# Waits of GpSimd on quarters of a weight buffer in a three-layer transformer kernel

## The reference

```python
for l in range(DEPTH):                    # first_block, DEPTH = 2
    h = rmsnorm(x, norm_w[l])
    proj = jnp.einsum("bsd,de->bse", h, w_in[l])       # 2048 -> 6160
    ...                                    # ssd, conformer, differential attention
    y = jnp.concatenate([y_ssd, y_cfm, y_att], axis=-1)
    x = x + jnp.einsum("bse,ed->bsd", y, w_out[l])
...
u = rmsnorm_2(h, g_pre)                   # hybrid_layer
z = u @ w_in                              # 2048 -> 9216
...                                       # banded attention, recurrence
y = jnp.concatenate([y_att, y_hg], axis=-1).astype(h.dtype) @ w_out
h = h + rmsnorm_2(y, g_post)
gate = jax.nn.sigmoid((h @ w_pg).astype(f32))
e = (p_l @ w_pp).astype(f32)
h = h + rmsnorm_2((gate * e).astype(h.dtype), g_ple)
```

## Time and profile before

| what | value |
| --- | --- |
| median of 3 runs | 3264.14 us (3263.51 to 3265.61) |
| span of the profiled execution, first to last instruction | 3255.8 us |
| the profiled execution's own time | not given beside its span |
| TensorE busy | 3045.4 us |
| GpSimd busy | 1950.9 us |
| VectorE busy | 1788.9 us |
| ScalarE busy | 954.7 us |
| mean granted TensorE clock | 0.971 of full speed |

### The profile page before, as it was taken

The page is one execution under the profiler, slowest core; times in us unless marked ns, Lnnn a source line. Parts: engine busy times, 40 slices in busy tenths (PEclk is TensorE's granted clock), DMA queues, the critical chain, the costliest instruction groups (busy, mean ns, idle before and its releaser), DMA issues.

```text
span 3255.8 us, 39402 instructions
## 1 busy us (share of the span) xinstructions
PE 3045.4 (94%) x15114; PEld 2371.9 (73%) x15114; DVE 1788.9 (55%) x2433; ACT 954.7 (29%) x1644; POOL 1950.9 (60%) x1860
## 2 busy tenths in 40 slices
PE   8999999989999999999999999999899998898997
PEld 5787777668778877776787677776677776686675
DVE  6754777741384568675218533334678887413313
ACT  5334213320124330333103232324454444301101
POOL 5566666547676656555557655554576765465551
PEclk9999999999999999999999999999999999999997
DMA  5232222233222222222432222222122221322221
GB/s 199 91 108 99 78 85 84 78 108 129 104 104 104 104 78 102 73 78 72 151 117 92 93 68 80 81 79 71 53 79 78 78 79 65 111 97 87 75 96 60
DMA packets 64140, 298.67 MB, mean 92 GB/s; under 512 B 6704, under 2 KB 11696, under 8 KB 34512
## 3 DMA queue, kind: packets, MB, share of 16 engines
q1 hardware_dynamic: 36384, 247.48, 21.9%
q10 hardware_dynamic: 27568, 48.67, 4.5%
HBM read 274.04 MB, written 16.84 MB: 89 GB/s over the span
## 4 chain that ended last, share of the span: by engine, by line
PE 67%; DVE 24%; ACT 6%; issue 2%; POOL 1%; ACTq 1%; DVEq 0%; DMA 0%; SPq 0%; POOLq 0%
PE bank L401 57%; DVE bank L1959 5%; DVE h_lo L1698 2%; DVE rec_ex L2295 1%; PE bank L729 1%; DVE norm_y L1737 1%; PE bank L746 1%; PE bank L738 1%; PE bank L919 1%; PE bank L822 1%; DVE newton L1677 1%; DVE last_z L2413 1%; PE bank L616 1%; DVE rec_lk L2308 1%; PE bank L797 1%
## 5 line engine op out<-in xcount | busy, mean ns | idle before, releaser
L401 PE MATMUL bank<-h_hi,w_lo 128*128 128x512 f32 x3712 | 1513.5, 408 | 79.0 <-DVE h_lo L1698 30.0
L401 PE MATMUL bank<-h_hi,w_hi 128*128 128x512 f32 x3712 | 1463.5, 394 | 0.0
L401 PE MATMUL bank<-h_lo,w_hi 128*128 128x512 f32 x3712 | 1462.6, 394 | 0.0
L2463 POOL TENSOR_SCALAR w_hi<-w_raw 128x512 fp32r<-128x512 f32 x928 | 692.3, 746 | 1168.0 <-PE bank L401 1105.9
L2465 POOL TENSOR_TENSOR w_lo<-w_raw,w_hi 128x512 fp32r<-128x512 f32 x928 | 1282.2, 1382 | 77.4
L401 PEld LDWEIGHTS bank<-h_hi,w_lo 128*128 128x128 f32 x3712 | 707.0, 190 | 302.1 <-issue 49.9
L401 PEld LDWEIGHTS bank<-h_hi,w_hi 128*128 128x128 f32 x3712 | 706.9, 190 | 153.5
L401 PEld LDWEIGHTS bank<-h_lo,w_hi 128*128 128x128 f32 x3712 | 708.2, 191 | 149.0 <-issue 10.6
L960 ACT ACTIVATE raw<-bank 128x512 f32<-128x512 f32 x148 | 88.5, 598 | 420.2 <-PE bank L401 363.6
L1959 DVE SCALAR_TENSOR_TENSOR bank<-cfm_up,par,bank 128x512 f32<-128x512 f32 x232 | 175.4, 756 | 8.3
L2127 DVE TENSOR_TENSOR xT<-bank,xT 128x512 f32<-128x512 f32 x32 | 22.1, 692 | 222.5 <-PE bank L401 222.0
(11 more groups left out here) (326 smaller groups left out, 2756.0 us busy)
## 6 DMA issues: line engine op xcount, KB each, us to landing
w_raw<-in_wall SPq DMA_DIRECT2D x230, 1024.0 KB, 4.9
x_scratch<-xT ACTq DMA_DIRECT2D x12, 1024.0 KB, 4.7
xT<-x_scratch ACTq DMA_DIRECT2D x12, 1024.0 KB, 7.4
ssd_abc<-acs_scratch ACTq DMA_DIRECT2D x16, 512.0 KB, 3.7
first_xin<-in_x SPq DMA_DIRECT2D x4, 1024.0 KB, 11.4
out<-last_rows ACTq DMA_DIRECT2D x4, 1024.0 KB, 4.2
w_raw<-in_wall SPq DMA_DIRECT2D x8, 256.0 KB, 10.3
att_tq<-att_uq ACTq DMA_DIRECT2D x32, 64.0 KB
```

Of the source, the lines that this page charges most:

```text
L401: mm = t.matmul(bank[BANK[u]][:, :], w[:, CS16[k]], h[:, k, :], start=(k == 0 and w is m.w_lo[b]), stop=(k == KT - 1 and w is m.w_hi[b] an ...
L2463: g.tensor_scalar(m.w_hi[b][:, part], m.w_raw[b][:, part], 1.0, 1.0, ALU.mult, ALU.mult).then_inc(*s.hi.inc(u, n))
```

## The change

GpSimd's order is written by a new function, `piece_order`: unit by unit, and in a pair quarter by quarter of the two units alternately, in the order in which TensorE reads them. The two units after a pair are no longer taken alternately unless they are a pair themselves. Ahead of every quarter from unit 2 on GpSimd waits for that quarter of unit `u - 2`, and for the last quarter for the end of that unit. For this TensorE increments its semaphore after the quarters 0, 1 and 2 of every unit that stands alone; in `behind` the increments stay as they were and are noted for both units. Units 0 and 1 of the three output products and of the gate product are now listed in `PAIRS`.

```diff
@@ -173,7 +173,20 @@
 PAIRS += [(("wo", l, KT - 2), ("wo", l, KT - 1)) for l in range(DEPTH)]
+PAIRS += [(("wo", l, 0), ("wo", l, 1)) for l in range(DEPTH + 1)] + [(("pg", 2, 0), ("pg", 2, 1))]
 PAIRED = frozenset(UNIT[pair[0]] for pair in PAIRS)
+
+
+def piece_order():
+
+    u, order = 0, []
+    while u < N_UNITS:
+        us = (u, u + 1) if u in PAIRED else (u,)
+        order += [(b, n) for n in range(PIECES) for b in us]
+        u += len(us)
+    return order
@@ -392,7 +405,7 @@
-    def tiles(u, lo, hi):
+    def tiles(u, lo, hi, alone=True):
@@ -400,6 +413,8 @@
+            if alone and k % 4 == 3 and k < KT - 1:
+                mm.then_inc(*pe.inc("piece", u, k // 4))
         if hi == KT:
             mm.then_inc(*s.unit.inc(u))
@@ -424,11 +439,12 @@
             for u in us:
-                mm = tiles(u, k, k + 1)
+                mm = tiles(u, k, k + 1, False)
             if k < KT - 1 and (free is not None or k % 4 == 3):
                 mm.then_inc(*pe.inc("free", free, k))
             if k < KT - 1 and k % 4 == 3:
-                pe.mark("piece", us[0], k // 4)
+                for u in us:
+                    pe.mark("piece", u, k // 4)
@@ -2465,23 +2481,14 @@
-    for n in range(PIECES):
-        for u in range(2):
+    for u, n in piece_order():
+        if u < 2:
             g.wait_ge(*s.piece[u][n].at("w"))
-            split(u, n)
-    u = 2
-    while u < N_UNITS:
-        us = (u, u + 1) if u in PAIRED or u - 2 in PAIRED else (u,)
-        for b in us:
-            g.wait_ge(*s.raw[b % 2].at(b))
-        for n in range(PIECES):
-            if u - 2 in PAIRED and n < PIECES - 1:
-                g.wait_ge(*s.pe.at("piece", u - 2, n))
-            elif n == 0 or u - 2 in PAIRED:
-                g.wait_ge(*s.unit.at(us[-1] - 2))
-            for b in us:
-                split(b, n)
-        u += len(us)
+        elif n == 0:
+            g.wait_ge(*s.raw[u % 2].at(u))
+        if u >= 2:
+            g.wait_ge(*(s.pe.at("piece", u - 2, n) if n < PIECES - 1 else s.unit.at(u - 2)))
+        split(u, n)
```

## The result

The changed kernel takes 3294.28 us (median of 4 runs, 3288.18 to 3297.45), the kernel before beside it 3264.61 (3263.51 to 3265.61). The ratio is 1.0088, with a 95% interval of 1.0074 to 1.0101: slower by 30 us, where 24 us less was forecast.

A forecast was written before the change was run, and what follows sets the result against it. TensorE, busy 94% of the span, was taken to bound the kernel, its chain 67% TensorE and 24% VectorE. Terms -13.4 - 4.7 - 12 + 6.5 = -23.6, taken as -24, gave 3240 us, range 3223 to 3257.

The forecast's parts named there:

- (a): Pair of units 14 and 15 of the output product, layers 0 and 1: stalls and lower clock go, 13.4 us saved.
- (b): Unit 2 of each output product, behind a pair: TensorE's three waits for GpSimd go, 4.7 us saved.
- (c): Start of the banded stage, 1740 to 1812: TensorE's 7.8 us of waits for GpSimd, worth nothing by themselves beside VectorE's queue.
- only the stalls go: Rival: low clock stays or VectorE's low parts become the limit, and collisions cancel; 3252 us, chance 0.19.
- fourteen low parts: VectorE's work for the next layer behind the pair of units 14 and 15: keeps up narrowly, 1.29 against 1.36 us.
- New marks, waits, fence at 0: TensorE's 615 increments, GpSimd's added waits and the moved `leave("decays")` fence: each taken to cost 0 us.
- The last head: Last head of the recurrence: fewer GpSimd bursts beside VectorE's instructions, -4.7 us and -1.5 for the next burst.
- The gate pair: Gate product's pair, where VectorE sets the pace: three GpSimd pieces now fall there, +2.5 us.
- bursts of 0.8 us are paid there too, and more would meet VectorE than now: +3: Attention: new collisions, priced from VectorE's narrow one-input step of 168 to 954 ns, cost 3 us.
- collision in step: Rival: in attention each quarter's end starts a split that meets VectorE's row step, 37 us; 3277 us, chance 0.07.
- With waits by quarter GpSimd works when TensorE reads and stops when TensorE stalls for VectorE.: Ground for fewer collisions in recurrence and the banded stage's start; collision relief sums to -12 us, bounds 0 and -25.
- A rule that was weighed and not used: Exclusion of VectorE and GpSimd for a whole instruction: a collision could cost 1.3 us, the new-collision sum +9 not +6.5.

The follow-up runs named there:

- e5: Kernel before with TensorE's marks, units 0 and 1 of the output products listed as pairs, quarter waits around listed pairs alone: 3249.64 us, ratio 0.9949.
- e1: Kernel before with TensorE's 615 new marks only and nothing that waits for them: 3265.17 us, ratio 1.0003.
- e4: Changed kernel, but GpSimd waits once for the whole unit in attention's units: 3270.65 us, ratio 1.0017.
- e7: Changed kernel's order and list of pairs, but whole-unit waits away from the pairs: 3246.38 us, ratio 0.9943.
- e9: Changed kernel with whole-unit waits away from pairs, gate pair not listed, every quarter waited for from unit 196 on: 3247.22 us, ratio 0.9941.
- e10: Changed kernel, but units 132 and 133 at the band's start are split alternately again, once both are loaded: 3297.12 us, ratio 1.0096.
- e2: Kernel before with GpSimd's splits cut to 32 of 512 columns from unit 2 on: 3139.76 us, ratio 0.9622.
- e3: Changed kernel with GpSimd's splits cut to 32 of 512 columns from unit 2 on: 3135.73 us, ratio 0.9607.

## Why the prediction was wrong

**Terms that held.** *(a) and (b)*: 13.4 + 4.7 = 18.1 us forecast. By units, (a) came to 7.2 us in layer 0 (units 50 to 69) and 6.6 in layer 1 (114 to 129), (b) to some 5 us. The outputs as a whole are 23.9 us shorter in the changed kernel and 19.3 in e5; most of the surplus, 3.5 us, lies at units 130 and 131, among the waits (c) that were called worth nothing, and it goes back in the next stage (below). The clock followed the stall, so that the rival "only the stalls go" is out, and VectorE's fourteen low parts kept up. *New marks, waits, fence at 0*: e1 shows the first and third; for the waits, TensorE waits for GpSimd for 1.5 us in all after the change. *The last head* (-4.7 and -1.5): 4.8 us measured. *The gate pair* (+2.5): +3.3. VectorE's row there, in the changed kernel:

```profile
3045.72 0.69 DVE L1714 TENSOR_TENSOR h_lo<-xT,h_hi 128x512 fp32r<-128x512 f32 x1
3046.45 0.98 DVE L2429 SCALAR_TENSOR_TENSOR last_z<-last_z,par,last_rs 128x512 f32<-128x512 f32 x1
3047.53 1.58 DVE L2439 TENSOR_TENSOR xT<-xT,last_z 128x512 f32<-128x512 f32 x1
```

A piece lengthens two instructions, 0.98 - 0.75 and 1.58 - 0.69, together 1.12 us; three pieces make 3.4.

**The step that failed: what new collisions cost in attention, "bursts of 0.8 us are paid there too, and more would meet VectorE than now: +3".** I took the price of a new collision in attention from one narrow step, and its median, 182 ns, as evidence that bursts seldom cost. That line is short, so it is seldom hit; the instructions around it that are 0.69 us long and come nine in a row I did not look at. The measured term is +22.8 us where +3 stood, and e4 gives it back by undoing the waits of attention alone. The rival "collision in step" had the right place and the right sign. Its mechanism was half right: not the 168 ns step, but VectorE's rows of 0.69 us, and attention stays long at all four positions of the mark, so the spreading of the pieces counts there rather than a coincidence with one moment. Its forecast of 3277 charged 37 us to attention, which lost 22.8; that the time came to 3294 all the same is the loss of the other stretches.

**"With waits by quarter GpSimd works when TensorE reads and stops when TensorE stalls for VectorE."** From this I took -3 for the other heads of the recurrence and -3 for the start of the banded stage. Measured: +9.7 and +8.5. The sentence holds for the last head, where TensorE stands still. Elsewhere TensorE's filler products run beside VectorE's rows, so marks come, and with them pieces, just while VectorE is what the end waits for. Of the recurrence's 9.7 us the 6.8 at units 165 to 167 are firm: they take 72.0 to 72.7 us in the profiles of before, e1, e5, e7 and e9, and 75.4 to 79.0 in those with quarter waits throughout and GpSimd's whole work. The other 2.9 are within what two executions differ by: over units 168 to 195 e1 took 399.2 us and the profile of before 391.0, with the same work.

**The place behind the pairs.** The start of layer 1 was forecast at +1 and measured at +4.0; e7, with whole-unit waits there, has none of it. The band's start hangs together with the gain itself. At the band's start e5 and e7, whose attention is as before, still show 39.2 and 40.0 us where e1 has 35.1: about 4 us of what the stage in front won is given back, since VectorE's normalisation sets the pace there. Layer 1's output product and the band's start together (units 112 to 133) take 275.7 us in e1, 268.0 in e5, 267.7 in e7 and 271.4 in the changed kernel. So the other 4 come with the quarter waits. Which of GpSimd's pieces does it stays open; e10 does not settle it.

**A rule that was weighed and not used.** The rows show first: behind GpSimd's 1.3 us instruction VectorE's 0.69 becomes 1.6, behind its 0.6 us instruction 0.98, and the line that reads one operand from PSUM keeps its 754 to 757 ns in both kernels, 232 times:

```profile
L1975 DVE SCALAR_TENSOR_TENSOR bank<-cfm_up,par,bank 128x512 f32<-128x512 f32 x232 | 175.4, 756 | 8.3
```

The Trainium skill (page "SBUF — State Buffer", section "Who interferes with whom") says that a VectorE instruction with two SBUF inputs and a GpSimd instruction that reads SBUF exclude each other, and that one with a single SBUF input outside the two-port modes does not take part; the traces agree in both. The prediction set this rule beside the price of one collision and did not count collisions by it. By rows the number was to be had: nine such instructions a head, three heads a layer in the stretch shown, 54 in all; if half are newly hit, at a mean of 0.6 us (between 0.29 and 0.9), that is an estimate of 16 us. Measured were 12 lengthened before and 43 after, and 9.9 + 10.2 = 20.1 us more in the two layers.

**The base.** 8.3 us around the span was 1.5 us and a quick execution of about 7. Against the medians it made no difference to the sign.

## What to carry to other kernels

Before a helper engine's work is spread more finely, count what runs beside it on the engine that it holds up: one long burst and a gap can be cheaper than four short bursts, since a row of dependent instructions is lengthened in most of its members where the gap is lost. Apply a finer wait only where the coarse one shows up as a wait on the path (here around the listed pairs: 3249.64 and 3246.38 us against 3264), and leave it out where the helper was early anyway. The typical duration of a short instruction says nothing about collisions; read the least and the median of the long ones in the row that the path follows.

## What the runs showed of the hardware

- The part of GpSimd's splitting that e2 and e3 leave out costs this kernel 125 us before and 159 us after, of 3264 and 3294, most of it through VectorE; without it the mean granted clock is 0.984, with it 0.971.
- An instruction of VectorE of 0.69 us with two SBUF inputs and one of GpSimd's that reads SBUF take turns: the later one ends its own length less some 0.15 us behind the other's end. The lengths seen most are 0.69, 0.91 to 0.98, 1.13, and 1.6 to 1.67. GpSimd's own instructions are lengthened in turn, 0.62 to 1.06 and 1.29 to 1.60.
- 615 additional semaphore increments on TensorE's products cost nothing that 10 runs can tell (1.0003, 0.9993 to 1.0012).
- One and the same kernel gives 3258.7 to 3268.1 us, and its recurrence 391 or 399 us in two profiles; one profile is not a base for terms of a few us.
